# Retention and the first delta-rule step of a two-block sequence kernel, reordered over the five engines

## The reference, cut to what matters

```python
# retention, per head and direction
R_i = gamma**C * R_{i-1} + sum_j gamma**(C-1-j) * k_j v_j^T
o_m = sum_{j<=m} gamma**(m-j) * (q_m . k_j) * v_j + gamma**(m+1) * q_m R_{i-1}
# gated delta rule, per head and direction
S_t = exp(g_t) (I - beta_t k_t k_t^T) S_{t-1} + beta_t k_t v_t^T,   o_t = S_t^T q_t
```

## Time and profile before

| what | value |
|---|---|
| median of the runs | 3481.64 us |
| the profiled execution | 3481.5 us |
| its span from first to last instruction | 3479.7 us |
| mean granted clock of TensorE, as a share of full speed | 0.992 |
| TensorE busy in the stretch 300 to 350 us | 43.11 us |
| TensorE busy in the stretch 350 to 400 us | 34.18 us |

### The profile page before, as it was taken

The page is one execution under the profiler, slowest core; times in us unless marked ns, Lnnn a source line. Parts: engine busy times, 40 slices in busy tenths (PEclk is TensorE's granted clock), DMA queues, the critical chain, the costliest instruction groups (busy, mean ns, idle before and its releaser), DMA issues.

```text
span 3479.7 us, 46745 instructions
## 1 busy us (share of the span) xinstructions
PE 3375.9 (97%) x17274; PEld 2844.0 (82%) x17274; DVE 1236.5 (36%) x1890; ACT 1367.0 (39%) x1910; POOL 1484.2 (43%) x1090
## 2 busy tenths in 40 slices
PE   6999899899999999999999999999999999999998
PEld 4777799788888888888888888888888888888887
DVE  6763577521123111645216111331126353151104
ACT  4444333544325432326524443254323264244423
POOL 2232000255544554454543554455544545545544
PEclk9999999999999999999999999999999999999999
DMA  6342000122222222222222322222222323223222
GB/s 259 127 146 67 1 1 1 67 97 96 97 97 91 96 96 97 86 98 94 100 96 73 109 96 97 85 97 96 96 97 91 98 85 108 94 72 108 96 97 97
DMA packets 90036, 322.21 MB, mean 93 GB/s; under 512 B 9776, under 2 KB 12208, under 8 KB 89776
## 3 DMA queue, kind: packets, MB, share of 16 engines
q1 hardware_dynamic: 88576, 316.64, 26.9%
q10 hardware_dynamic: 1328, 3.67, 0.3%
HBM read 318.18 MB, written 2.10 MB: 92 GB/s over the span
## 4 chain that ended last, share of the span: by engine, by line
issue 55%; POOL 33%; PE 10%; DVE 1%; POOLq 1%; ACT 0%; DMA 0%; DVEq 0%; SPq 0%; ACTq 0%
POOL w_lo L456 33%; PE ps L485 2%; PE ps L481 2%; PE ps L480 2%; PE ps L994 1%; PE ps L999 1%; PE ps L992 1%; PE ps L1018 0%; PE ps L1022 0%; PE ps L1016 0%; POOLq L454 0%; DVE X L2002 0%; POOLq L123 0%; PE ps L937 0%; DVE ps L2024 0%
## 5 line engine op out<-in xcount | busy, mean ns | idle before, releaser
L456 POOL TENSOR_TENSOR w_lo<-raw,w_hi 128x512 fp32r<-128x512 f32 x1086 | 1484.0, 1388 | 1987.2 <-ACT w_hi L1164 1987.1
L1164 ACT ACTIVATE w_hi<-raw 128x1024 fp32r<-128x1024 f32 x543 | 575.5, 1060 | 1459.6 <-PE ps L485 897.8
L480 PE MATMUL ps<-acts,w_hi 128*128 128x512 f32 x2776 | 1080.1, 389 | 0.1
L481 PE MATMUL ps<-acts,w_hi 128*128 128x512 f32 x2776 | 1080.0, 389 | 0.0
L485 PE MATMUL ps<-acts,w_lo 128*128 128x512 f32 x2776 | 685.6, 389 | 0.0
L480 PEld LDWEIGHTS ps<-acts,w_hi 128*128 128x128 f32 x2776 | 521.1, 188 | 108.4 <-ACT tmp L1518 0.5
L485 PEld LDWEIGHTS ps<-acts,w_lo 128*128 128x128 f32 x2776 | 521.1, 188 | 108.1
L481 PEld LDWEIGHTS ps<-acts,w_hi 128*128 128x128 f32 x2776 | 521.2, 188 | 108.0
L2072 DVE TENSOR_TENSOR tmp<-tmp,ps 128x512 f32<-128x512 f32 x110 | 75.7, 688 | 787.6 <-PE ps L485 727.4
L992 PE MATMUL ps<-acts,w_hi 128*128 (+1 forms) x440 | 171.2, 389 | 0.0
L994 PE MATMUL ps<-acts,w_hi 128*128 (+1 forms) x440 | 171.2, 389 | 0.0
(11 more groups left out here) (382 smaller groups left out, 4123.6 us busy)
## 6 DMA issues: line engine op xcount, KB each, us to landing
raw<-stream SPq DMA_DIRECT2D x543, 512.0 KB, 3.3
ada_behind<-ada SPq DMA_DIRECT2D x32, 512.0 KB, 3.6
ada_first<-ada SPq DMA_DIRECT2D x8, 1024.0 KB, 13.3
X<-x_in ACTq DMA_DIRECT2D x1, 2048.0 KB, 8.4
out<-X SPq DMA_DIRECT2D x16, 128.0 KB, 1.8
xin<-x_in ACTq DMA_DIRECT2D x2, 768.0 KB, 6.9
xin<-x_in SPq DMA_DIRECT2D x2, 768.0 KB, 9.0
rope_sb<-rope SPq DMA_DIRECT2D x1, 1280.0 KB, 9.0
```

Source lines behind the costliest of these rows:

```text
L456: last = nc.gpsimd.tensor_tensor(w_lo[:, slot, part, :], raw[:, slot % RAW, part, :], f32(w_hi[:, slot, part, :]), ALU.subtract)
L480: mm(o, w_hi[:, s, k, :], xh, start=start, stop=False, skip_group_check=True)
L481: mm(o, w_hi[:, s, k, :], xl, start=False, stop=False, skip_group_check=True)
L1164: A(w_hi[:, s, :, :], raw[:, s % RAW, :, :], ACT.Copy).then_inc(s_hi, 1)
```

## The change

It does the following.

- **Opening.** The two constants that the sums need are loaded before the modulation weights; the third load (`cst1`) comes after the third weight chunk, with a semaphore of its own (`s_fixed`). The sums of squares stand after six of the first eight `part_chunk`s. The second part's rows are copied half by VectorE and half by ScalarE, ahead of ScalarE's first two `hi_part`s.
- **Projections.** VectorE's `part_rows` stands one item earlier, after the wait for that item's eviction and before its convolution. The turn of "ab" comes after the first two token tiles of the values (tiles 2 and 3 are computed first).
- **Retention.** ScalarE evicts each token tile of the values as it is complete and scales the keys of steps 0 and 1 between them, with three of four weight chunks done before; the fourth comes after them. GpSimd decays the queries. The query-key product is a step ahead, in a bank that alternates. Key-value products stand between the outputs of the two directions. ScalarE, not VectorE, copies the first four outputs. `decay_rows(0)`, `key_products(0)` and the rest of the first delta-rule step's preparation stand within the last three retention steps; the decays `gt[d][0]` get memory of their own, and odd and even steps change their sets of buffers. ScalarE's squares of `oret` (before L1314) stand after `decays(0)`.
- **Delta rule.** At level 2 VectorE does both directions' L1877 and then both right sides; before, the second right side was at level 3.

```diff
@@ sync @@
-            load_first(0)
-            load_first(1)
             sp.dma_start(ident[:, :], consts[:, 0:P]).then_inc(s_cst, 16)
             sp.dma_start(ones[:, :], consts[:, P:2 * P]).then_inc(s_cst, 16)
-            for n in range(2, FIRST):
+            for n in range(FIRST):
                 load_first(n)
-            sp.dma_start(cst1[:, :, :].rearrange("p a n -> p (a n)"), consts[:, 2 * P:5 * P]).then_inc(s_cst, 16)
...
+                if n == 2:
+                    sp.dma_start(cst1[:, :, :].rearrange("p a n -> p (a n)"), consts[:, 2 * P:5 * P]).then_inc(s_fixed, 16)
@@ gpsimd @@
+            def decayed_queries(s):
+                for d in range(2):
+                    c = order[d][s]
+                    if s > NCC:
+                        pool.wait_ge(s_rod[d], s - NCC)
+                    nc.gpsimd.tensor_tensor(rt[3 + d][:, :, :], rqT[:, :, c * P - CTX:(c + 1) * P - CTX],
+                                            rt[5 + d][:, :, :], ALU.mult).then_inc(s_rqx[d], 1)
...
+            for slot in range(SLOTS - 1 + N_PROJ % SLOTS):
+                low_part(slot % SLOTS)
+            pool.wait_ge(s_fin, n_aux[-1])
+            pool.wait_ge(s_sil, 3 * H)
+            pool.wait_ge(s_dexp, 1)
+            decayed_queries(NCC)
+            low_part((N_PROJ + SLOTS - 1) % SLOTS)
+            for s in range(NCC + 1, NC):
+                decayed_queries(s)
...
@@ tensor @@
-            for n in range(KT):
-                part_chunk(n, n // KT)
-            pe.wait_ge(s_cst, 48)
+            for n in range(KT - 2):
+                part_chunk(n, 0)
+            pe.wait_ge(s_cst, 32)
             pe.wait_ge(s_sqadd, KT)
...
+            for s in range(2):
+                key_values(s, 0)
+                key_values(s, 1)
+                turn(2 * NC + 2 * s)
+                turn(2 * NC + 2 * s + 1)
+            pe.wait_ge(s_rv, NC)
+            query_keys(NCC)
+            for s in range(NCC, NC):
+                outputs(s, 0)
+                if s < NC - 1:
+                    key_values(s, 0)
+                    query_keys(s + 1)
+                outputs(s, 1)
+                if s < NC - 1:
+                    key_values(s, 1)
+                if s == NCC:
+                    turn(2 * NC + 4)
+                    turn(2 * NC + 5)
+                if s == NCC + 1:
+                    pe.wait_ge(s_turned, len(turned))
+                    decay_rows(0)
+                if s == NCC + 2:
+                    key_products(0)
...
                         pe.wait_ge(s_gyc[d], 6 * s + lev)
+                        if s == 0 and lev == 1:
+                            pe.wait_ge(s_ro[d], NC - NCC)
@@ scalar @@
+            for q in (2, 3):
+                last = A(arow[0:2, 2 * P * q:2 * P * (q + 1)], ps[1][32 * q:32 * q + 2, 0:2 * P], ACT.Copy)
+            last.then_inc(s_arow2, 1)
             for _ in range(RAW):
                 hi_part()
...
+            for t in range(NC):
...
+                A(rvtok[:, t, :], ps[t][:, :], ACT.Copy).then_inc(s_rv, 1)
+                if t in (2, 4):
+                    scaled_keys(t // 2 - 1)
+            hi_part()
+            scaled_keys(2)
+            scaled_keys(3)
+            first_outputs(NCC, 0)
+            first_outputs(NCC, 1)
+            scaled_keys(4)
+            first_outputs(NCC + 1, 0)
+            first_outputs(NCC + 1, 1)
...
             differences(0)
             decays(0)
+            act.wait_ge(s_turned, len(turned))
+            for d in range(2):
+                act.wait_ge(s_ro[d], 4)
+            for h in range(H):
+                A(tmp[h][:, :], oret[:, h, :], ACT.Square).then_inc(s_hrsq, 1)
@@ vector @@
-                if i in TURNS:
-                    part_rows(TURNS[i], 6)
+                if i < n and items[i][0] in CONV + ROPED:
+                    dve.wait_ge(s_pread, i + 1)
+                if i + 1 in TURNS:
+                    part_rows(TURNS[i + 1], 6)
...
+            for s in range(NCC, NC - 1):
+                for d in range(2):
+                    if s > NCC + 1:
+                        added_outputs(s, d)
+                    new_state(s, d)
+                    if d == 0:
+                        masked_products(s + 1)
+                if s == NCC:
+                    copy_turn(2 * NC + 4)
+                    copy_turn(2 * NC + 5)
+                if s == NCC + 1:
+                    for d in range(2):
+                        dve.wait_ge(s_rkz[d], NC - 1)
+                    unit(0)
             for d in range(2):
                 negative_matrix(0, d)
             pairs(0)
+            dve.wait_ge(s_rod[0], NC - NCC)
+            turned_pairs(0, 0)
+            dve.wait_ge(s_rqx[1], NC - NCC)
+            turned_pairs(0, 1)
             for d in range(2):
-                turned_pairs(0, d)
+                added_outputs(NC - 1, d)
...
-                        if s and lev == 2 + d:
+                    if s and lev == 2:
+                        for d in range(2):
                             right_side(s, d)
```

More of the change, by code:

```diff
@@ L518, in _ @@
             mm(ps[5][:, :], ones[:, :], big[2][:, CTX:TOK], start=True, stop=True).then_inc(s_ss, 1)
[L519 removed]
+            for n in range(KT - 2, KT + 4):
                 part_chunk(n, n // KT)
@@ L595, in _ @@
                         last.then_inc(s_aux_done, 1)
[L596 to L600, removed]
-                                                       pbuf(j)[0:16, c * P:(c + 1) * P], ident[0:16, 0:16])
-                        last.then_inc(s_abt, 1)
             def turn(j):
@@ L623, in _ @@
                 pe.wait_ge(s_lo, n_lo.up())
-                for t in range(NC):
+                for n, t in enumerate((2, 3, 0, 1, 4, 5) if q == 0 else range(NC)):
+                    if (q, n) == (0, 2):
+                        turn_ab()
                     for kk in range(2):
@@ L687, in _, with key_values @@
-            pe.wait_ge(s_turned, len(turned))
-            pe.wait_ge(s_ro[1], 4)
-            pe.wait_ge(s_ro[0], 4)
-            pe.wait_ge(s_rS[0], NC - 1)
-            pe.wait_ge(s_rS[1], NC - 1)
+            def key_values(s, d):
+                c = order[d][s]
+                pe.wait_ge(s_rkz[d], s + 1)
+                if s:
+                    pe.wait_ge(s_rS[d], s)
+                for h in range(H):
+                    last = mm(ps[4 * d + 2][:, h * P:(h + 1) * P], zbuf(d, s)[:, h, :], rvtok[:, c, h * P:(h + 1) * P],
+                              start=True, stop=True)
+                last.then_inc(s_rkv[d], 1)
@@ new lines, in query_keys, with outputs @@
+            def query_keys(s):
+                c = order[0][s]
+                for h in range(H):
+                    last = mm(ps[rqk_bank(s)][:, h * P:(h + 1) * P], rkT[:, h, c * P:(c + 1) * P],
+                              rqT[:, h, c * P - CTX:(c + 1) * P - CTX], start=True, stop=True)
+                last.then_inc(s_rqk, 1)
+            def outputs(s, d):
+                c = order[d][s]
+                if d == 0:
+                    pe.wait_ge(s_rm, s - NCC + 1)
+                pe.wait_ge(s_rqx[d], s - NCC + 1)
+                if s > NCC:
+                    pe.wait_ge(s_ro[d], s - NCC)
+                pe.wait_ge(s_rS[d], s)
+                for h in range(H):
+                    o = ps[4 * d + 1][:, h * P:(h + 1) * P]
+                    last = mm(o, retS[d][:, h, :], rt[3 + d][:, h, :], start=True, stop=(d == 1))
+                    if d == 0:
+                        last = mm(o, rvtok[:, c, h * P:(h + 1) * P], rt[2][:, h, :], start=False, stop=True)
+                last.then_inc(s_rod[d], 1)
@@ new lines, in new_state @@
+            def new_state(s, d):
+                b = 4 * d
+                dve.wait_ge(s_rkv[d], s + 1)
+                if s == 0:
+                    CP(flat(retS[d]), ps[b + 2][:, :]).then_inc(s_rS[d], 1)
+                else:
+                    for h in range(H):
+                        last = STT(retS[d][:, h, :], retS[d][:, h, :], gch[:, 4 * d + h:4 * d + h + 1],
+                                   ps[b + 2][:, h * P:(h + 1) * P], ALU.mult, ALU.add)
+                    last.then_inc(s_rS[d], 1)
```

177 lines of the change are left out of this document (83 added, 94 removed).

## The result

| | before | after |
|---|---|---|
| median of 4 runs, alternating on one chip | 3481.77 us | 3436.11 us (3435.87 to 3437.14) |
| span of the profiled execution | 3479.7 us | 3434.4 us |
| mean granted clock | 0.992 | 0.994 |

The ratio is 0.9868, 95% interval 0.9851 to 0.9885: faster by 1.3%, well over 0.2%. The direction was right and the size was not: 45.3 us came off the span where 37.4 were forecast.

What follows compares the result with a forecast made beforehand. TensorE, busy 97% of the span, bounds the kernel, so only its idle or low-clock time can be won. Terms 1.0 - 5.2 - 1.9 - 26.4 - 4.9 = -37.4 us gave 3444 us, range 3436 to 3458.

Steps and rivals of the forecast that it cites:

- Delta-rule order: Delta rule, VectorE's order: earlier decay rows and no level 5 wait for the merge, -4.9 us (bounds -6 and -2).
- Retention and the first delta step: Last projection to level 2: waits gone, one mask wait, new wait behind squares; 66.8 us becomes 38.7 + 1.7, -26.4.
- The bound without the clock: Retention and first delta step: -28.1 us if no lower clock follows the gap behind ScalarE's squares.
- Opening: Start of kernel: coefficients about 2.6 us earlier, 3.9 given back to GpSimd overlap; taken as +1.0 us (bounds -3.4, +2).
- rival 1: Opening: GpSimd and VectorE interleave without loss, giving -3.4 us and not +1.0, 3440 us; chance 0.12.
- Projections and gates: Projections: wait for the rows' copy at item 13 and lower clock gone, -5.2 us; gates' eviction wait covered, -1.9.
- Rival 2: Retention: TensorE waits 3.0 us at each of four steps for other engines' hand-overs, +12, 3456 us; chance 0.18.
- Rival 3: Retention: TensorE's 29.7 us run at half the clock, +30, 3474 us; chance 0.04.
- rival 4: Projections: the rows' copy gains nothing, TensorE being held at another item, 3449 us; chance 0.04.
- Rival 5: Retention: GpSimd's product of t sets the step at 2t + 2.7; with t = 10 us slower, 3495 us; chance 0.02.

Runs made afterwards that it cites:

- e2: Changed kernel with the query-key product times decay of both directions at level 2, ahead of both right sides, as the prediction had read it: 3440.7 us, ratio 0.9874.
- e9: Changed kernel with only the opening put back (load order, sums behind all first-part products, rows copied by VectorE alone): 3438.82 us, ratio 0.9870.
- e4: Changed kernel with VectorE's copy of the modulation rows one item later, as before the change: 3441.77 us, ratio 0.9878.
- e11: Changed kernel with the gates' turn back behind the last projection and token tiles in natural order: 3437.71 us, ratio 0.9868.
- e7: Changed kernel with both directions' outputs ahead of the first direction's key-value products in each retention step: 3436.55 us, ratio 0.9871.
- e5: Changed kernel with each of GpSimd's query products done twice, same result: 3435.77 us, ratio 0.9865.
- e6: Changed kernel with each of GpSimd's query products done four times, same result: 3449.19 us, ratio 0.9905.
- e8: Changed kernel with the queries decayed by VectorE instead of GpSimd: 3438.16 us, ratio 0.9873.
- e1: Changed kernel with VectorE's delta-rule order as before (query-key product times decay at level 2, second right side at level 3): 3444.8 us, ratio 0.9888.
- e10: Changed kernel with ScalarE's first high part ahead of its two copies of the modulation rows: 3435.60 us, ratio 0.9862.

## Why the prediction was wrong in size, point by point

- **Delta-rule order: the step that failed.** "the second direction's decay rows start 0.73 us later than the first's end ... because a right side stands ahead of L1877", and with it the -4.9, priced an order that the kernel does not have. The arithmetic was good: that order, run in e2, brings 5.1. The changed kernel also moves L1877 to level 1, which removes the waits of TensorE for it altogether (1.6 us) and takes 1.1 off that of the last step; together with 1.1 that no wait names it is 3.8 more. The term measured is -9.0 for -4.9, beyond its bound of -6, and 4.1 of the missing 7.9 us (45.3 less 37.4). The other misses are 2.7 in the retention and 1.3 in the opening, less 0.2 in the projections.
- **Retention and the first delta step: right in mechanism, 2.7 short.** The wait of 4.9 is gone, the groups run back to back at 0.89 us, the mask's wait is 0.8 for 1.0. I had added 1.7 us of lower clock behind the squares' gap, and the clock did not fall in this execution, which is luck: behind the same gap it fell in three of nine other profiles. The remaining 1.0 is 0.6 of a shorter gap (2.50 for 3.1) and small sums. The bound without the clock (-28.1) was passed by 1.0. That the clock gives back up to 8.8 of the 29.1 us is in the prediction's sum, since it priced every group at the full clock, but it did not set it apart.
- **Opening: +1.0 forecast, -0.3 measured (and -2.8 against e9).** The sums come at 20.80 instead of 25.39, and the coefficients start at 38.22, 2.45 earlier than before (2.6 forecast). VectorE and GpSimd, of after:

```profile
38.22 0.99 DVE L1711 SCALAR_TENSOR_TENSOR coef<-mod,prm 128x8 f32<-128x8 f32 x2
39.25 1.24 DVE L1718 TENSOR_SCALAR big<-xin,coef,mod 128x256 f32<-128x256 f32 x1
40.41 1.48 DVE L1719 TENSOR_SCALAR big<-xin,coef,mod 128x512 f32<-128x512 f32 x1
41.81 1.35 DVE L1718 TENSOR_SCALAR big<-xin,coef,mod 128x256 f32<-128x256 f32 x1
43.09 0.53 DVE L1719 TENSOR_SCALAR big<-xin,coef,mod 128x512 f32<-128x512 f32 x1
```

```profile
37.85 5.17 POOL L459 TENSOR_TENSOR w_lo<-raw,w_hi 128x512 fp32r<-128x512 f32 x4 [37.40 <-ACT w_hi L1213]
```

While GpSimd works, L1718 takes 1.24 and 1.35 us and L1719 1.48, alone 0.41 and 0.53. So the overlap is paid, and rival 1 (no loss, 3.4 gained) is out. But three of the four overlaps are new, and the stretching adds 0.58 + 0.95 + 0.95 = 2.5 us, less 0.2 for a wait for ScalarE that is gone. I had 3.9, a whole instruction of GpSimd for each. The Trainium skill, "SBUF — State Buffer", section "Who interferes with whom", says that VectorE and GpSimd share a pair of SBUF ports, and that whoever issues first holds it for the whole instruction. The prediction took its sentence on two SBUF inputs; L1718 and L1719, which stretch most, read one SBUF tile, and the same section counts `tensor_scalar` among those that can take the pair. The trace agrees that the two engines stretch one another (e9: 9.18 for 7.04 as well). The stretches of 0.58 to 0.95 us, each less than GpSimd's 1.26, fit a loser that waits only for what is left of the other's instruction; no run shows that by itself.
- **Projections and gates: right.** -6.9 against -7.1; e4 gives the first as 5.3 (5.2 forecast), and in e11's trace the second's wait of 1.9 us is back (1.9).
- **Rivals.** Rival 2 (hand-overs, +12) did not occur: TensorE does not wait in steps 3 to 5 even where the order is another (e7) or the product twice as long (e5). Rival 3 (clock, +30) did not occur. Rival 1 (no loss in the opening) is out by the stretched instructions above, rival 4 by e4. Rival 5's mechanism exists (e6), at 1.27 us it is far away, and its formula was 2.7 us too dear a step.

The terms as measured, 0.3 + 6.9 + 29.1 + 9.0, make the 45.3. Open is why the clock falls behind one gap and not behind another of the same length: e2, e4 and e8 had it behind the 2.49 us, after, e1, e5, e7, e9, e10 and e11 not. No run varied that by itself.

## What to carry to other kernels

Before an order of instructions is priced, write out what each engine does at each level, from the changed code itself; one instruction per direction a level earlier was worth 3.8 us here. When side work is put in front of an eviction on an in-order engine, ask what the side work waits for: four squares cost TensorE 2.5 us, and one move frees them. In the step chain TensorE stopped where it wanted a result of VectorE right after asking for it; with other groups put between, it ran on, and its clock stayed up, which gave up to 8.8 us more. Which engine takes the small products and in which order mattered by 2 us of 29.

## What was unexpected in the hardware

- The clock behind short gaps is not the same from execution to execution. After 1.9 us of idle time it stayed at 1.00 in before and fell to 0.50 in e11; after 2.49 to 2.50 us it stayed in after, e1, e5, e7, e9, e10 and e11 and fell in e2, e4 and e8 (0.72 from 364 to 368 us in e2). Each fall costs 1.4 to 1.7 us (in e2 the two groups behind the gap take 5.31 us, in after 3.87), so removing a short wait of TensorE is worth more than its length in some executions.
- In e9 the first sums took 1.22 us instead of 0.70 though the granted clock in the windows around them is 1.00, so a row's duration can double with no sign of it in that column. The modulation products show the same: 1.94 us in before and 1.07 in after, both begun at 19.73 us in windows of 1.00, while after's take 1.93 in windows of 0.50 (33.99 us). The durations look like the lower level; that it was the clock is not shown.
- GpSimd multiplies two 128x512 float32 tiles in 1.27 us, as long as it subtracts them (1.26); VectorE takes 0.69 for the same product before (L1786).
